# The FFN weights of a transformer block, laid out by quads in memory

## The chip, the cores and the metric

One NeuronCore of one Trainium2 chip runs the whole kernel. The metric is the time of one execution on the device in microseconds (us), the median of several runs. Its engines are TensorE (PE; its weight loads are listed apart as PEld), VectorE (DVE), ScalarE (ACT), GpSimd (POOL) and SyncE (SP); sixteen DMA engines move data between the main memory (HBM) and the on-chip memory, and they serve the queues of SP and POOL alike.

## The reference

One block with 256 tokens of width 2048, all in float32: a mixer of two kinds of attention, an output projection, and a feed-forward network (FFN) of width 5632. Only the last needs to be seen here:

```python
D_FF = -(-8 * D_MODEL // (3 * 256)) * 256          # 5632
...
    h = h + merged @ w_out[l]
    hn = rms_norm(h, norm_ffn_g[l])
    h = h + (jax.nn.silu(hn @ w_ffn_gate[l]) * (hn @ w_ffn_up[l])) @ w_ffn_down[l]
```

`w_ffn_gate` and `w_ffn_up` are 2048 x 5632, `w_ffn_down` is 5632 x 2048: 138 MB in all, each byte read once.

## The kernel before

**Products.** The kernel keeps the accuracy of float32 with three matmuls on a faster format. Each weight is split into a high and a low part (`u_hi`, made by ACT in L1134; `u_lo`, made by DVE in L1675), the activations likewise, and high by high, high by low (L2226, L2227) and low by high (L2231) are added in PSUM. The function `product` (L2220) does this for one unit: eight matmuls with the high part of the weights, then, after a wait on `lo_ready`, four with the low part, each with 128 x 512 weights moving past a loaded block of activations.

**Units, quads and panels.** A quad is the raw float32 block that one load brings: 4 row tiles of 128 rows, by 512 columns (`UNIT_KT = 4`, `COLS = 512`), 1 MB, held as 128 partitions of 8 KB. Six buffers `quad0` to `quad5` take them in turn. A unit is a quad, or a sum of quads, that is split and multiplied. A panel is a pair of column blocks of 512 over 2048 rows. Its first 2 x 2 quads (11, 12, 21, 22) are multiplied by a Strassen-like scheme with seven products, the units M1 to M7; the remaining four quads are the plain units N0 to N3, each multiplied by both halves of the tokens. The sums of quads that the scheme needs are made on DVE (L1683, L1689, L1694) and, one for each panel, by an accumulating DMA that POOL issues (L918, `quad<-quad`): quad 22 is added onto quad 12, for unit M7. The FFN has 17 panels: 11 of kind `gu`, whose two halves are the same column block of gate and up, and 6 of kind `down`, in three blocks (4, 4 and 3 `gu` panels, after each two `down` panels). The order of the units is written out by hand (`ORDER`, `SHORT_ORDER`); `plan_panels` builds the panels from the number of column blocks of the FFN, and `plan_loads` gives each load its buffer and the event that frees it.

**Loads.** The weights come on SP's queue. `load_quad` (issue in L815) first waits until DVE has made the low part, or the last sum, of what lay in the buffer (`quad_freed`), then issues one DMA. Its source is the weight matrix as the caller has it, rows apart by the full width of the matrix; the view `(k p) n -> p k n` makes partition p take row p of each of the four row tiles:

```python
                src = w[0, row0:row0 + UNIT_KT * P, col0:col0 + COLS].rearrange("(k p) n -> p k n", p=P)
                sp.dma_start(panel.stage.quad[slot][:].rearrange("p (k n) -> p k n", n=COLS), src).then_inc(panel.stage.landed[slot], 16)
```

So a partition reads four runs of 512 floats (2 KB). On SP nothing but further loads stands behind an FFN load, and after the last of them the read of the partial output (L860). ACT waits for the landing in `unit_hi` (L1134), DVE in its sums, POOL before L918.

**The other DMAs of this stage.** The results of the `down` panels leave PSUM through ACT (`evac`, L1299) and POOL adds them to the output in memory by accumulating DMAs (L947, `out<-evac`). The residual h is loaded once as 2 MB, x in rows of 8 KB (L853).

Of the kernel before, what the change touches and what calls it, by code (L numbers as in the profile page):

```python
# [27 lines left out]
P = 128  # L28
COLS = 512
# [9 lines left out]
UNIT_KT = 4  # L39
# [165 lines left out]
def single(kind, col, kt, letter="O"):  # L205

    panel = Panel(-1, kind, col, kt, None)
    for i in range(kt // UNIT_KT):
        panel.add_unit(f"{letter}{i}", f"{letter}{i}", i * UNIT_KT)
    return panel  # L210


def plan_out(kt, n, first_index):

    third_out = single("out", 2, kt, "U")
    panel = Panel(n, "out2", 0, kt, None)
    panel.i = -1
    panel.add_products()
    for a, name in enumerate(OUT_ORDER):
        u = (third_out if name[0] == "U" else panel).unit[name]  # L220
        u.index = first_index + a
        panel.order.append(u)
    return third_out, panel
# [44 lines left out]
def plan_panels(kt, ff_cols, d_cols, first_index, first_n):  # L268

    last_out = single("out", d_cols - 1, kt)  # L270
    panels = []

    def panel(kind, col, kts):
        panels.append(Panel(first_n + len(panels), kind, col, kts, panels[-1] if panels else None))
        panels[-1].i = len(panels) - 1
        panels[-1].add_products()
        return panels[-1]

    down = 0
    for block, ff in enumerate(range(0, ff_cols, FF_BLOCKS)):  # L280
        k = min(FF_BLOCKS, ff_cols - ff)
        for i in range(k):
            p = panel("gu", ff + i, kt)
            p.block, p.block_slot = block, i
        for m in range(d_cols // 2):
            p = panel("down", m, k * GROUP)
            p.block, p.row, p.down = block, ff * GROUP, down
            down += 1
    index = first_index
    for p in panels:  # L290
        short = p.kind == "down" and p.col == 0 and p.kts < kt
        for name in SHORT_ORDER if short else ORDER if p.i else FIRST_ORDER:
            owner = p.prev if name[-1] == "-" else last_out if name[0] == "O" else p
            if name[0:2] in owner.unit:
                p.order.append(owner.unit[name[0:2]])
        if p is panels[-1]:
            p.order += [p.unit[name] for name in ("N2", "N3") if name in p.unit]
        for u in p.order:
            u.index = index
            index += 1  # L300
    return last_out, panels
# [54 lines left out]
def build(nc, x, norm_mix_g, w_in, q_norm_a, k_norm_a, sink_a, t5_bias, q_norm_b, k_norm_b, rel_bias_b,  # L356
# [3 lines left out]
    KT = D // P  # L360
    NB = D // COLS
# [11 lines left out]
    PIECES = jobs[-1].piece0 + jobs[-1].pieces  # L373
# [10 lines left out]
    last_slots = dict(zip(b_units[-4:], ((3, 1), (2, 0), (0, 2), (3, 0))))  # L384
    b_hi_free, b_lo_free = plan_splits(b_units, B0, B0, B0 + 4, (), B0 + 4, last_slots)
    third_out, outs = plan_out(KT, len(heads) + len(branches), PIECES)
    last_out, panels = plan_panels(KT, w_ffn_gate.shape[2] // COLS, NB, PIECES + len(outs.order), outs.n + 1)
    units = outs.order + [u for panel in panels for u in panel.order]
    loads, _ = plan_loads(units, [PIECES - 2 * RAW_SLOTS + 2 * slot + 2 for slot in range(RAW_SLOTS)] + [0, 1])
    H_SETS = 1 + max(j.set for j in jobs if j.set is not None)  # L390
# [10 lines left out]
    with ExitStack() as ctx:  # L401
# [319 lines left out]
        def _(sp):  # L721
# [3 lines left out]
            def quad_freed(freed):  # L725
                if freed[0] == "sum":
                    sp.wait_ge(sum_ready, sums(freed[1], "Z"))
                else:
                    sp.wait_ge(lo_ready, freed[1] + 1)
# [47 lines left out]
            def load_quad(load):  # L777

                panel, name, slot, freed = load.panel, load.name, load.slot, load.freed
                if freed is None and panel.stage is q_stage:  # L780
                    if slot < RAW_SLOTS:
                        sp.wait_ge(lo_ready, 2 * RAW_SLOTS + 2 * slot + 2)
                elif freed is None and panel.stage is b_stage:
                    if slot < RAW_SLOTS:
                        sp.wait_ge(lo_ready, B0 - 2 * RAW_SLOTS + 2 * slot + 2)
                    else:
                        sp.wait_ge(piece_used, B0)
                elif freed is None:
                    if slot < RAW_SLOTS:
                        sp.wait_ge(lo_ready, PIECES - 2 * RAW_SLOTS + 2 * slot + 2)  # L790
                    else:
                        sp.wait_ge(piece_used, after_branch.piece0)
                else:
                    quad_freed(freed)
                if panel.kind == "out":
                    w, row0, col0 = w_out, load.kt0 * P, panel.col * COLS
                elif panel.kind == "out2":
                    w, row0, col0 = w_out, load.kt0 * P, (2 * panel.col + load.half) * COLS
                elif panel.kind == "v":
                    w, row0, col0 = w_in, load.kt0 * P, head_col("v", panel.col)  # L800
                elif panel.kind == "gb":
                    w, row0, col0 = w_in, load.kt0 * P, QA + 2 * KVA + 3 * QB + D + panel.col * COLS
                elif panel.kind == "ba":
                    w, row0, col0 = w_branch_a, load.kt0 * P, (2 * panel.col + load.half) * COLS
                elif panel.kind == "heads":
                    w, row0 = w_in, load.kt0 * P
                    col0 = head_col(*panel.halves[load.half])
                elif panel.kind == "gu":
                    w, row0 = (w_ffn_gate, w_ffn_up)[load.half], load.kt0 * P
                    col0 = panel.col * COLS  # L810
                else:
                    w, row0 = w_ffn_down, (panel.row + load.kt0) * P
                    col0 = (2 * panel.col + load.half) * COLS
                src = w[0, row0:row0 + UNIT_KT * P, col0:col0 + COLS].rearrange("(k p) n -> p k n", p=P)
                sp.dma_start(panel.stage.quad[slot][:].rearrange("p (k n) -> p k n", n=COLS), src).then_inc(panel.stage.landed[slot], 16)  # L815

            def head_col(kind, n):

                if kind == "v":
                    return QA + 2 * KVA + 2 * QB + n * COLS  # L820
                return n * COLS if n < QA // COLS else 2 * KVA + n * COLS

            def do_job(j):
                if j is jobs[2]:
                    for load in q_loads:
                        load_quad(load)
                if j is after_branch:
                    for c, load in enumerate(b_loads):
                        load_quad(load)
                        i = att_step(jobs[2], 2 * c + B0 - ATT_PIECE0, 6)  # L830
                        if i // 2 < NATT:
                            load_bias(i // 2)
                for q in range(j.pieces // 2):
                    if j.prev is None:
                        load_first(j, 2 * q)
                        load_first(j, 2 * q + 1)
                    else:
                        load_chunk(j, q)
                    i = att_step(j, 2 * q, 6)
                    if i >= 0 and i // 2 < NATT:  # L840
                        if i == 0:
                            sp.wait_ge(table_stored, 16)
                            sp.wait_ge(masks_ready, 1)
                        load_bias(i // 2)
# [4 lines left out]
            for c, load in enumerate(loads):  # L849
                load_quad(load)  # L850
                if c == H_AFTER:
                    sp.wait_ge(merged, NB)
                    sp.dma_start(h[:], x_view).then_inc(h_landed, 16)  # L853
# [1693 lines left out]
    return (np.arange(buckets)[:, None] == bucket[None, :]).astype(np.float32)  # L2547


# [14 lines left out]
```

## Time and profile before

| | us |
|---|---|
| median of 3 runs | 1275.11 (1274.64 to 1275.16) |
| the profiled execution | 1275.66 |
| its span, first to last instruction | 1273.9 |
| PE busy | 1267.6 |
| DVE busy | 1041.1 |
| ACT busy | 749.8 |
| granted TensorE clock | 1.0 of full speed throughout |

The profile lists every instruction with its start and duration, the DMA packets, and for each idle stretch of an engine the event that ended it. Busy times overlap between engines. Matmuls are pipelined: their records are longer (0.39 us) than the distance from one to the next, so for PE it is the distance that tells the pace.

### The profile page before, as it was taken

The numbers are of one execution on the slowest core, as the hardware profiler recorded it, in microseconds if no ns is written. First come the engines' busy times: TensorE is split into PE (matmuls) and PEld (weight loads), VectorE is DVE, ScalarE is ACT, GpSimd is POOL, SyncE is SP. The second block draws the span as 40 slices with busy tenths as digits, with TensorE's granted clock in tenths as the row PEclk, the third lists the DMA queues.
The fourth block names the chain that finished last, engine by engine and source line by source line (L and its number), as shares of the span: only waits on it lengthen the run. The fifth ranks groups of instructions, "written<-read, shape, count | busy, mean of one in ns | idle before, by whom it ended". The sixth has DMA issues, their size and how long they took to land.

```text
span 1273.9 us, 15071 instructions
## 1 busy us (share of the span) xinstructions
PE 1267.6 (100%) x5925; PEld 1044.0 (82%) x5925; DVE 1041.1 (82%) x932; ACT 749.8 (59%) x761; POOL 80.6 (6%) x71
## 2 busy tenths in 40 slices
PE   9999999999999999999999999999999999999999
PEld 7888887777788888888888888888888888888887
DVE  5888787778897577868989887878898888888996
ACT  5776566665675454556656655656565655556653
POOL 1212230000000000001000000000000001000000
DMA  7876747553675766956786669877877689866874
GB/s 250 306 230 201 238 129 228 156 155 119 191 252 174 242 224 206 320 208 186 243 278 218 201 196 287 256 244 207 260 227 252 185 245 285 253 213 195 282 219 121
DMA packets 137589, 282.88 MB, mean 222 GB/s; under 512 B 5344, under 2 KB 13856, under 8 KB 134320
## 3 DMA queue, kind: packets, MB, share of 16 engines
q1 hardware_dynamic: 130624, 250.37, 56.6%
q0 software_dynamic: 6896, 31.55, 13.1%
q8 instruction: 47, 0.77, 0.2%
q14 instruction: 22, 0.18, 0.0%
HBM read 249.38 MB, written 8.41 MB: 202 GB/s over the span
## 4 chain that ended last, share of the span: by engine, by line
PE 95%; DVE 2%; ACT 1%; issue 1%; DMA 0%; POOL 0%; SPq 0%; DVEq 0%; ACTq 0%
PE bank L2226 25%; PE bank L2231 25%; PE bank L2227 25%; PE bank L2166 6%; PE bank L2167 5%; PE bank L2174 5%; PE bank L2115 1%; DVE u_lo L1675 1%; PE bank L2142 1%; PE bank L2384 1%; PE bank L2127 1%; DMA x_rows<-in_x 0%; PE bank L2100 0%; ACT u_hi L1134 0%; PE bank L2090 0%
## 5 line engine op out<-in xcount | busy, mean ns | idle before, releaser
L1675 DVE TENSOR_TENSOR u_lo<-quad,u_hi 128x2048 fp32r<-128x2048 f32 x237 | 538.5, 2288 | 107.0 <-ACT u_hi L1134 57.1
L1134 ACT ACTIVATE u_hi<-quad 128x2048 fp32r<-128x2048 f32 x242 | 459.9, 1915 | 276.5 <-PE bank L2231 154.5
L2226 PE MATMUL bank<-u_hi,xT_hi 128*128 128x512 f32 x644 | 251.0, 390 | 0.0
L2227 PE MATMUL bank<-u_hi,xT_lo 128*128 128x512 f32 x644 | 250.6, 389 | 0.0
L2231 PE MATMUL bank<-u_lo,xT_hi 128*128 128x512 f32 x696 | 186.3, 389 | 0.0
L2231 PEld LDWEIGHTS bank<-u_lo,xT_hi 128*128 128x128 f32 x696 | 130.5, 188 | 27.4 <-DVE u_lo L1675 0.3
L2226 PEld LDWEIGHTS bank<-u_hi,xT_hi 128*128 128x128 f32 x644 | 120.9, 188 | 25.3 <-issue 0.3
L2227 PEld LDWEIGHTS bank<-u_hi,xT_lo 128*128 128x128 f32 x644 | 120.9, 188 | 25.0
L1430 DVE TENSOR_TENSOR w_lo<-raw,w_hi 128x1024 fp32r<-128x1024 f32 (+1 forms) x80 | 92.9, 1170 | 53.2 <-ACT w_hi L979 51.3
L979 ACT ACTIVATE w_hi<-raw 128x1024 fp32r<-128x1024 f32 (+1 forms) x80 | 80.4, 1016 | 89.5 <-PE bank L2174 77.2
L2166 PE MATMUL bank<-w_hi,xT_hi 128*128 128x512 f32 (+1 forms) x256 | 99.4, 392 | 0.0
L2167 PE MATMUL bank<-w_hi,xT_lo 128*128 128x512 f32 (+1 forms) x256 | 95.7, 378 | 0.0
L2227 PE MATMUL bank<-u_hi,fT_lo 128*128 128x512 f32 (+1 forms) x236 | 90.7, 385 | 0.0
L2226 PE MATMUL bank<-u_hi,fT_hi 128*128 128x512 f32 (+1 forms) x236 | 90.7, 385 | 0.0
L2226 PE MATMUL bank<-u_hi,xs_hi 128*128 128x512 f32 x216 | 85.0, 394 | 0.7 <-DVE bank L1705 0.7
L2227 PE MATMUL bank<-u_hi,xs_lo 128*128 128x512 f32 x216 | 84.1, 389 | 0.0
L918 POOL DMA_DIRECT2D quad<-quad x23 | 20.4, 886 | 825.9 <-DVE quad L1683 639.8
L2174 PE MATMUL bank<-w_lo,xT_hi 128*128 128x512 f32 (+1 forms) x256 | 65.2, 377 | 0.0
L2231 PE MATMUL bank<-u_lo,fT_hi 128*128 128x512 f32 (+1 forms) x236 | 62.2, 385 | 0.0
L2231 PE MATMUL bank<-u_lo,xs_hi 128*128 128x512 f32 x224 | 59.9, 389 | 0.0
L2166 PEld LDWEIGHTS bank<-w_hi,xT_hi 128*128 128x128 f32 x256 | 48.2, 188 | 10.3 <-issue 0.6
L2167 PEld LDWEIGHTS bank<-w_hi,xT_lo 128*128 128x128 f32 x256 | 48.3, 189 | 7.8
(277 smaller groups left out, 1845.8 us busy)
## 6 DMA issues: line engine op xcount, KB each, us to landing
quad<-in_w_ffn_gate SPq DMA_DIRECT2D x44, 1024.0 KB, 6.8
quad<-in_w_ffn_up SPq DMA_DIRECT2D x44, 1024.0 KB, 6.2
quad<-in_w_ffn_down SPq DMA_DIRECT2D x44, 1024.0 KB, 6.2
quad<-in_w_in SPq DMA_DIRECT2D x33, 1024.0 KB, 6.4
raw<-in_w_in SPq DMA_DIRECT2D x24, 1024.0 KB, 5.6
quad<-quad POOLq DMA_DIRECT2D x23, 1024.0 KB, 8.2
quad<-in_w_out SPq DMA_DIRECT2D x16, 1024.0 KB, 6.0
raw<-in_w_branch_b SPq DMA_DIRECT2D x8, 1024.0 KB, 5.3
```

Source lines behind the costliest of these rows:

```text
L918: pool.dma_start(st.quad[panel.slot["12"]][:], st.quad[panel.slot["22"]][:], accum_op=ALU.add).then_inc(q_summed, 16)
L979: A(w_hi[:, p % SPLIT_SLOTS, 0:w], raw[:, c % RAW_SLOTS, (k % 2) * w:(k % 2 + 1) * w], ACT.Copy).then_inc(hi_ready, 1)
L1134: A(st.hi[u.hi][:], st.quad[slot][:], ACT.Copy).then_inc(hi_ready, u.step)
L1430: V.tensor_tensor(w_lo[:, p % SPLIT_SLOTS, 0:w], raw[:, (j.chunk0 + k // 2) % RAW_SLOTS, (k % 2) * w:(k % 2 + 1) * w], w_hi[:, p % SPLIT_S ...
L1675: V.tensor_tensor(st.lo[u.lo][:], st.quad[u.panel.slot[u.raw]][:], st.hi[u.hi][:].bitcast(F32), ALU.subtract).then_inc(lo_ready, u.step)
L2115: ins = M(dst, qT[rows, b * PAIRS + n, tokens(t)], k, start=True, stop=True)
L2166: M(sums, hi[:, j.kt0 + kt, tokens(t)], w_hi[:, p % SPLIT_SLOTS, w], start=kt == 0, stop=False)
L2167: M(sums, lo[:, j.kt0 + kt, tokens(t)], w_hi[:, p % SPLIT_SLOTS, w], start=False, stop=False)
L2174: ins = M(sums, hi[:, j.kt0 + kt, tokens(t)], w_lo[:, p % SPLIT_SLOTS, w], start=False, stop=kt == j.kts - 1)
L2226: M(sums, a_hi(k), hi[:, w], start=start and k == 0, stop=False, skip_group_check=True)
L2227: M(sums, a_lo(k), hi[:, w], start=False, stop=False, skip_group_check=True)
L2231: ins = M(sums, a_hi(k), lo[:, w], start=False, stop=k == UNIT_KT - 1, skip_group_check=True)
```

## The change

The three FFN weights are passed as arrays of another shape, made on the host before the launch: (column blocks of 512, row quads of 512 rows, 128, 2048). Entry [c, r, p] holds, one behind the other, row p of each of the four row tiles of quad (c, r). `load_quad` takes one such entry for a `gu` or `down` panel and copies it as it lies: 128 partitions of 8 KB, 1 MB in one piece. The number of column blocks of the FFN, formerly the width by 512, is read from the first size of the new array. All other weights are loaded as before.

```diff
@@ -384,7 +384,7 @@
-    last_out, panels = plan_panels(KT, w_ffn_gate.shape[2] // COLS, NB, PIECES + len(outs.order), outs.n + 1)
+    last_out, panels = plan_panels(KT, w_ffn_gate.shape[0], NB, PIECES + len(outs.order), outs.n + 1)
@@ -806,11 +806,14 @@
                 elif panel.kind == "gu":
-                    w, row0 = (w_ffn_gate, w_ffn_up)[load.half], load.kt0 * P
-                    col0 = panel.col * COLS
+                    sp.dma_start(panel.stage.quad[slot][:], (w_ffn_gate, w_ffn_up)[load.half][panel.col, load.kt0 // UNIT_KT]
+                                 ).then_inc(panel.stage.landed[slot], 16)
+                    return
                 else:
-                    w, row0 = w_ffn_down, (panel.row + load.kt0) * P
-                    col0 = (2 * panel.col + load.half) * COLS
+                    sp.dma_start(panel.stage.quad[slot][:],
+                                 w_ffn_down[2 * panel.col + load.half, (panel.row + load.kt0) // UNIT_KT]
+                                 ).then_inc(panel.stage.landed[slot], 16)
+                    return
@@ -2547,6 +2550,13 @@
+def by_quad(w):
+
+    rows, cols = w.shape
+    tiles = w.reshape(rows // (UNIT_KT * P), UNIT_KT, P, cols // COLS, COLS).transpose(3, 0, 2, 1, 4)
+    return np.ascontiguousarray(tiles.reshape(cols // COLS, rows // (UNIT_KT * P), P, UNIT_KT * COLS))
...
+        if name in ("w_ffn_gate", "w_ffn_up", "w_ffn_down"):
+            a = by_quad(a[0])
```

## Rows read from the trace of the kernel before

**Rows 1.** The page, busy time of each engine, share of the span, instructions.
```profile
PE 1267.6 (100%) x5925; PEld 1044.0 (82%) x5925; DVE 1041.1 (82%) x932; ACT 749.8 (59%) x761; POOL 80.6 (6%) x71
```
**Rows 2.** Windows: length, busy PE, PEld, DVE, ACT, POOL, clock, DMA share, GB/s.
```profile
540.00:1274.00 734.00, 730.96 (x3294) 606.22 (x3292) 620.28 (x363) 426.65 (x314) 30.91 (x33) 1.00 0.73 229
1100.00:1125.00 25.00, 25.00 (x112) 20.71 (x111) 18.17 (x9) 13.61 (x12) 2.09 (x2) 1.00 1.05 326
1255.00:1270.00 15.00, 15.00 (x76) 12.74 (x75) 8.62 (x9) 1.71 (x1) 1.21 (x1) 1.00 0.36 75
```
**Rows 3.** Chain of waits in time, 1104 to 1113 us: start, length, what.
```profile
1106.43 0.91 PE bank L2231 x4
...
1109.15 0.91 PE bank L2231 x4
```
**Rows 4.** The same chain, 1256 to 1266 us.
```profile
1256.39 0.91 PE bank L2231 x4
...
1259.11 0.91 PE bank L2231 x4
```
**Rows 5.** The chain by line, 540 us to the end.
```profile
by line: PE bank L2231 32.6%; PE bank L2226 32.6%; PE bank L2227 32.5%; PE bank L2384 1.3%; PE bank L2397 0.5%; DVE part L2046 0.1%; issue 0.0%
```
**Rows 6.** Waits of PEld, 540 us to the end: total, times, longest.
```profile
PEld bank L2226 <- issue: 0.7, 2, 0.5
```
**Rows 7.** Waits of SP's queue, same stretch and columns.
```profile
SPq L815 <- DVE u_lo L1675: 643.7, 117, 16.2
```
**Rows 8.** L815, 540 to 1274 us (ns of an issue, landings); last, the load at 611.4.
```profile
L815 SPq DMA_DIRECT2D quad<-in_w_ffn_gate x43: 367/368/368, 563.1 to 1162.4; - x43
...
DMA to landing us min/median/max: 4.9/6.3/12.1
...
DMA to landing us min/median/max: 8.6/8.6/8.6
```
**Rows 9.** Timeline of ACT, DVE and PE around that load's unit: start, length.
```profile
620.07 1.92 ACT L1134 ACTIVATE u_hi<-quad 128x2048 fp32r<-128x2048 f32 x1
617.51 6.81 DVE L1675 TENSOR_TENSOR u_lo<-quad,u_hi 128x2048 fp32r<-128x2048 f32 x3
631.15 0.84 PE L2231 MATMUL bank<-u_lo,xT_hi 128*128 128x512 f32 x3
```
**Rows 10.** The page's DMA issues: KB each, median us to landing.
```profile
quad<-in_w_ffn_gate SPq DMA_DIRECT2D x44, 1024.0 KB, 6.8
quad<-quad POOLq DMA_DIRECT2D x23, 1024.0 KB, 8.2
h<-in_x SPq DMA_DIRECT2D x1, 2048.0 KB, 7.4
```
**Rows 11.** The page's DMA packets and queues: packets, MB, share of 16 engines.
```profile
DMA packets 137589, 282.88 MB, mean 222 GB/s; under 512 B 5344, under 2 KB 13856, under 8 KB 134320
q1 hardware_dynamic: 130624, 250.37, 56.6%
q8 instruction: 47, 0.77, 0.2%
q14 instruction: 22, 0.18, 0.0%
```
**Rows 12.** Landing of L918's at 1112.5; of all of L947; waits for L947.
```profile
DMA to landing us min/median/max: 10.0/10.0/10.0
...
DMA to landing us min/median/max: 5.7/10.7/12.7
...
ACT side_a L1281 <- DMA out<-evac: 7.9, 2, 4.0
```
**Rows 13.** Timeline of ACT, DVE and PE around that panel's M7: start, length.
```profile
1126.95 1.91 ACT L1134 ACTIVATE u_hi<-quad 128x2048 fp32r<-128x2048 f32 x1
1132.08 2.28 DVE L1675 TENSOR_TENSOR u_lo<-quad,u_hi 128x2048 fp32r<-128x2048 f32 x1
1139.83 0.85 PE L2231 MATMUL bank<-u_lo,xs_hi 128*128 128x512 f32 x3
```

## The prediction, made before the change was run

> **What bounds the kernel now.** I read the page from the top, then only the second half of the run, since that is where the changed loads are issued. The busy times come first [rows 1]: the matmul stream of TensorE (PE) covers 1267.6 of 1273.9 us, and no other engine is near that. A busy PE can still hide small holes, so the next thing to look at is the pace. In the chain of waits, followed in order of time, groups of four low-part matmuls stand 2.72 us apart while the DMA engines are at their busiest [rows 2, 3] (1106.43 and 1109.15). With the eight matmuls of the high part in between, twelve take 2.72 us, or 227 ns each. In the last 20 us, when no more weights are loaded, the same groups stand at 1256.39 and 1259.11 [rows 4]: 2.72 us again. The DMA share was 1.05 in the first stretch and 0.36 in the second [rows 2]. The pace of PE thus doesn't depend on what the DMA engines do.
>
> Next, who PE waits for. From 540 us to the end the chain is PE for 32.6 + 32.6 + 32.5 + 1.3 + 0.5 = 99.5% [rows 5]; no DMA is named in it. In the same stretch the list of waits has for the PE side one line: 0.7 us in all, in two pieces, released by no DMA [rows 6]. The loads themselves wait: SyncE's queue (SP), which issues them, spent 643.7 of these 734 us until VectorE (DVE) had finished with a buffer [rows 7]. The supply is paced by the consumer.
>
> How far ahead the supply runs is the cover that hides everything below. I looked for the load that leaves the least. It is the one issued at 611.4 us (panel 0, unit N3), which took 8.6 us to land [rows 8], so it was there at 620.0. ScalarE (ACT) began the unit's high part at 620.07 and ended at 621.99; DVE's run of three low parts, of which this unit's is the last, ended at 624.32; PE began the unit's low products at 631.15 [rows 9], and its eight high ones, at 0.227 us each, 1.8 us before, at 629.3. The load has 0.0 us to spare against ACT, yet the split weights lie ready 7.3 us (high) and 6.8 us (low) before PE asks for them. The slowest landing of the whole stage, 12.1 us [rows 8], belongs to no unit that is closer than this.
>
> **The change part by part.** What is computed, the order of units, buffers and waits stay as they are: the first size of the new gate array is the number of column blocks, which is what the old expression gave (5632 / 512 = 11). Only the source side of 132 loads (44 for each of the three weights [rows 10]) is another. Each still moves 1 MB and ends in one count on the same semaphore.
>
> Packets: a load of a quad has 128 partitions times 4 runs of 2 KB, 512 packets; laid out by quads it has 128 runs of 8 KB. That a run of 8 KB goes as one packet is borne out by a count: 137589 packets in all less 134320 under 8 KB leave 3269 [rows 11]. The 23 sums between two quads (128 partitions of 8 KB) make 2944, the one load of h (2 MB in rows of 8 KB) 256, the two instruction queues 47 + 22 = 69; together 3269 exactly [rows 10, 11]. So the hardware queue loses 132 x (512 - 128) = 50688 packets: 130624 become 79936.
>
> Time of a load: now 4.9 to 12.1 us, median 6.3 [rows 8]. The nearest row for runs of 8 KB from memory on the same queue is the load of h, 2 MB in 7.4 us [rows 10]; it too reads one contiguous block. If the rate per byte is that of the 2 KB runs, the quickest 1 MB load (4.9) and this one give 2.5 us for a further MB and 2.4 us that don't depend on size; that is a consistent pair, and it would leave the landing at 4.9 at best. If nothing were fixed, 1 MB would take 3.7. So a load gains between nothing and 1.2 us of its quickest time; I take the end near nothing, since 2.5 us per MB is already far quicker than the 326 GB/s that the busiest stretch reaches [rows 2]. The median should come to 5 to 6.3 us. On the path this is worth 0: the loads' landing is hidden by the 6.8 us and more of split weights ahead of PE [rows 9]. The cover would be gone if a load took 6.8 us longer than now, and then it would cost the excess.
>
> Issue: one instruction of 0.37 us per load on SP now [rows 8]. With a simpler pattern it costs between nothing and that. SP waits 643.7 us in the stage [rows 7], so 132 x 0.37 = 49 us saved or doubled vanish in its waits. Behind a load on SP stand only further loads and, at the end, the read of the partial output; a quicker issue starts nothing earlier, since each load is released by DVE.
>
> DMA time: the hardware queue's packets take 56.6% of 16 engines' span, 0.566 x 16 x 1273.9 / 130624 = 88 ns each [rows 11]. The changed loads have 67584 of them, 5970 us of engine time or 29% of the span. With the quickest load's 4.9 going to between 4.9 and 3.7, the share falls by 0 to 7 points; I expect 53 to 57% for the queue. PE doesn't wait for it: 0.
>
> The queue beside it: GpSimd (POOL) issues the sums of two quads (accumulating DMAs, 8.2 us to landing [rows 10]) and the sums into the output (10.7 us [rows 12]). They share the 16 engines with the loads, and the loads' pieces are now four times as large. At worst a sum stands behind one whole further load, 4.9 us. The sum issued at 1112.5 landed 10.0 us later, at 1122.5 [rows 12]; its reader, ACT's high part of M7, began at 1126.95, DVE ended the low part at 1134.36, and PE came to it at 1139.83 [rows 13]. The sum may be 4.4 us later before ACT notices, and DVE's result lies ready for 5.5 us more: cover 9.9 us against 4.9. The 17 quad sums of the stage are like it. The sums into the output held ACT up at one of its two lines for 7.9 us in all, at most 4.0 [rows 12], and such waits come out of the same lead of ACT over PE, 6.8 us and more, where 4.9 fits. Cost 0.
>
> The sum: against the profiled execution, 1273.9 us of span and 1.8 us around it make 1275.66. Change 0.0 from landings, 0.0 from issue, 0.0 from the other queue. That execution is 0.55 us above the median of the runs, 1275.11, so I forecast **1275.1 us**. What is left to come and go is the little that isn't pace: at most the 0.7 us of waits [rows 6] down, and about 1 us up for a unit that comes late once.
>
> **The rivals.**
> *Faster: the pace of PE has memory waits in it.* Of 734.0 us the weight loads of PE are busy for 606.2 [rows 2], which leaves 127.8 us. If these were waits for memory that the DMA engines cause, they would shrink with the DMA time, at most by 1.2 / 4.9 = 24%: 31 us, 1244 us. Against it stands the equal pace of 2.72 us at DMA shares of 1.05 and 0.36 [rows 2 to 4]; this alone holds such an effect under 0.01 us in 2.72. A gain of over 0.2% (2.6 us, about what a measurement of this kernel can tell from no change) would need a mechanism that I don't see. Chance 2%. The Trainium skill has the rule that makes this worth a rival: Perfetto Trace Analysis, Identifying the Most-Contended Engine, holds the matmul's busy time for a bad measure and wants the busy share of the weight loads judged instead. By that rule the kernel has 18% of headroom, not 0%. The trace has the 82%, and no wait in it that a DMA ends.
>
> *Slower: larger packets hold up the accumulating DMAs.* With 8 KB on either side a sum that alternates with loads gets a smaller share of an engine. It decides from the point where a quad sum lands 9.9 us later than now, 18 us and not 8.2. At 12 us later it would cost 2.1 us for each of the 17 panels of this stage, 36 us: 1311 us. For it: ACT already waits for these DMAs [rows 12]. Against it: a load has 1 MB in all, so no more than 4.9 us can be put ahead of a sum unless two loads are queued together, and 9.8 us is still within the cover. Chance 2%. The Trainium skill, in DMA: Bandwidth & Descriptors, Queues, rings and completion order, says that a DMA engine goes round its queues packet by packet; that is the mechanism by which larger packets would shift the shares. The trace of before doesn't show it one way or the other.
>
> *The change doesn't do what it says.* The contiguous 8 KB could be cut up again, or the block of 1 MB be spread over the engines in another way. Then the packets stay at 130624 and the landings at 6.3 us, or fall elsewhere between 5 and 12 us, and the time is the same 1275.1. Chance 3%.
>
> **How the numbers follow.** The forecast has 93%, the case of unchanged packets 3%, faster 2%, slower 2%. The first two are both no change: 96%. The range need not reach to the rivals: 0.7 us down and 1 us up from the terms above, and the spread of the runs (1274.64 to 1275.16) doubled, give 1273.9 to 1276.6.
>
> **What would show it.** In the profile of the changed kernel the hardware queue should have 79936 packets, the packets under 8 KB should be 66736, the landings of the FFN weights should be no longer than now, and the groups of four should still stand 2.72 us apart. The chain from 540 us on should be PE for over 99%. I am wrong if PE's pace in the FFN differs from 2.72 us, if PE or its weight loads wait for DVE or ACT by more than 2 us in all, or if the quad sums land more than 9.9 us later.

## The result, and the profile after

The changed kernel takes 1279.70 us (median of 6 runs, 1279.25 to 1283.6) against 1275.13 for the kernel before (6 runs, 1274.64 to 1275.78). The ratio is 1.0039, 95% interval 1.0029 to 1.005: 4.6 us or 0.4% slower. The forecast was no change, with a range that ended at 1276.6. Five of the six runs lie between 1279.25 and 1280.04; the sixth, 1283.6, is the only one whose mean granted TensorE clock is under 1.0 (0.999); `same_place_runs` below has more on that.

The table below puts the profiled execution of the changed kernel beside that of the kernel before. Its lines have moved: L815 became L809 (gate, up) and L813 (down), L918 is L921, L947 is L950, L1281 is L1284, L1299 is L1302, L2226 and L2231 are L2229 and L2234.

| | before | after |
|---|---|---|
| span, us | 1273.9 | 1278.2 |
| the profiled execution, us | 1275.66 | 1280.04 |
| PE busy, us | 1267.6 | 1268.3 |
| hardware queue: packets, share of 16 engines | 130624, 56.6% | 79936, 54.2% |
| output sums `out<-evac`, median to landing, us | 10.7 | 12.2 |

First the page of the changed kernel: its packets and queues. The 79936 packets of the hardware queue and the 66736 under 8 KB are the numbers worked out beforehand from [rows 11].

```profile
DMA packets 86901, 282.88 MB, mean 221 GB/s; under 512 B 5344, under 2 KB 13856, under 8 KB 66736
...
q1 hardware_dynamic: 79936, 250.37, 54.2%
```

Next the landings in the stage of the FFN. The first line is of the loads of gate and up (L809), the second of those of down (L813), the third of the quad sums (L921), the last of the output sums (L950).

```profile
DMA to landing us min/median/max: 4.7/6.3/9.6
...
DMA to landing us min/median/max: 4.7/5.5/9.6
...
DMA to landing us min/median/max: 7.9/8.7/10.0
...
DMA to landing us min/median/max: 5.8/12.2/13.4
```

The slowest loads became quicker (12.1 to 9.6 us) and the quickest a little (4.9 to 4.7); the median was 6.3 us over all loads [rows 8] and is now 6.3 for gate and up and 5.5 for down. The output sums, which the change doesn't touch, became 1.5 us slower ([rows 12] had 5.7/10.7/12.7).

The waits from 540 us on, with total, times and longest, are the lines that tell where the time went:

```profile
ACT side_a L1284 <- DMA out<-evac: 13.2, 2, 6.7
ACT evac L1302 <- DMA out<-evac: 10.9, 2, 5.6
PEld bank L2229 <- issue: 4.8, 6, 1.7
PE bank L2229 <- issue: 2.5, 2, 1.3
```

ACT waited 7.9 us for output sums in the first of these lines before [rows 12], and 13.2 now. The second line stood like this in the kernel before:

```profile
ACT evac L1299 <- DMA out<-evac: 7.2, 2, 3.8
```

The weight loads of PE, which had 0.7 us of waits in two pieces [rows 6], have 4.8 in six, and the matmuls 2.5 in two. (The two lines lie over each other: a hole in the one is a hole in the other.) The chain of waits, by line and then in order of time, names the two longest holes:

```profile
by line: PE bank L2229 32.6%; PE bank L2234 32.5%; PE bank L2230 32.4%; PE bank L2387 1.3%; PE bank L2400 0.5%; issue 0.4%; DVE part L2049 0.1%
...
867.90 1.29 issue
1118.34 1.22 issue
```

Here is the first of them in the timeline, start and length in us. In the kernel before, the output sum issued at 854.1 landed after 10.6 us, and this followed:

```profile
864.78 0.69 ACT L1281 ACTIVATE side_a<-bank,h_rs 128x512 f32<-128x512 f32 x1 [3.86 <-DMA out<-evac]
...
865.99 1.07 PE L2231 MATMUL bank<-u_lo,xT_hi 128*128 128x512 f32 x4
866.90 0.39 PE L2226 MATMUL bank<-u_hi,xT_hi 128*128 128x512 f32 x1
```

In the changed kernel the same sum was issued at 855.0 and landed after 13.4 us:

```profile
868.41 0.69 ACT L1284 ACTIVATE side_a<-bank,h_rs 128x512 f32<-128x512 f32 x1 [6.65 <-DMA out<-evac]
...
866.84 1.07 PE L2234 MATMUL bank<-u_lo,xT_hi 128*128 128x512 f32 x4
869.20 0.47 PE L2229 MATMUL bank<-u_hi,xT_hi 128*128 128x512 f32 x1 [1.29 <-issue]
```

The reader is to see two things. ACT's instruction is `gate_opened`: it reads PSUM bank 0 of the finished panel into `side_a`. Since `side_a` shares its memory with `evac`, the tile that the output sum is being read from, ACT must wait for the sum's landing. PE begins the next panel in bank 0 and waits until ACT has read it (`gate_ready`). And the cover there was small: before, ACT was done at 864.78 + 0.69 = 865.47 and PE came at 866.90; after, PE followed 0.10 us behind ACT's end (869.10 and 869.20). So a delay of 1.43 - 0.10 = 1.3 us would have cost nothing, and the sum landed 2.8 us later. At the other three places of the same sort (output sums issued near 814, 1064 and 1105 us) it is the same wait, in two of them with `evac` itself as the tile to be emptied into (L1302). Before, ACT and then PE at these three:

```profile
823.95 0.60 ACT L1299 ACTIVATE evac<-bank 128x512 f32<-128x512 f32 x1 [3.84 <-DMA out<-evac]
826.10 0.39 PE L2226 MATMUL bank<-u_hi,xT_hi 128*128 128x512 f32 x1
...
1071.96 0.60 ACT L1299 ACTIVATE evac<-bank 128x512 f32<-128x512 f32 x1 [3.40 <-DMA out<-evac]
1074.54 0.39 PE L2226 MATMUL bank<-u_hi,xT_hi 128*128 128x512 f32 x1
...
1113.38 0.69 ACT L1281 ACTIVATE side_a<-bank,h_rs 128x512 f32<-128x512 f32 x1 [4.02 <-DMA out<-evac]
1115.34 0.39 PE L2226 MATMUL bank<-u_hi,xT_hi 128*128 128x512 f32 x1
```

After, ACT alone; PE came at 826.84, 1077.25 and 1119.55, 0.10 us behind ACT's end each time:

```profile
826.14 0.60 ACT L1302 ACTIVATE evac<-bank 128x512 f32<-128x512 f32 x1 [5.37 <-DMA out<-evac]
...
1076.55 0.60 ACT L1302 ACTIVATE evac<-bank 128x512 f32<-128x512 f32 x1 [5.57 <-DMA out<-evac]
...
1118.77 0.69 ACT L1284 ACTIVATE side_a<-bank,h_rs 128x512 f32<-128x512 f32 x1 [6.57 <-DMA out<-evac]
```

The cover isn't the same at each place. It is the distance from ACT's end to PE's start before, less the 0.10 us that stays:

| output sum issued near | ACT waits longer by, us | cover, us | over the cover, us |
|---|---|---|---|
| 814 | 5.37 - 3.84 = 1.53 | 1.55 - 0.10 = 1.45 | 0.08 |
| 854 | 6.65 - 3.86 = 2.79 | 1.43 - 0.10 = 1.33 | 1.46 |
| 1064 | 5.57 - 3.40 = 2.17 | 1.98 - 0.10 = 1.88 | 0.29 |
| 1105 | 6.57 - 4.02 = 2.55 | 1.27 - 0.10 = 1.17 | 1.38 |

Together that is 3.2 us in this pair of executions, nearly all of it at the two places of `side_a`.

The two transfers that traded places can be seen side by side. The load of `up` issued 0.3 us after that output sum took 11.5 us before and 8.7 us after; the sum took 10.6 and 13.4. Before, the load and then the sum:

```profile
DMA to landing us min/median/max: 11.5/11.5/11.5
...
DMA to landing us min/median/max: 10.6/10.6/10.6
```

After, in the same order:

```profile
DMA to landing us min/median/max: 8.7/8.7/8.7
...
DMA to landing us min/median/max: 13.4/13.4/13.4
```

### The profile page after: what moved, and what is told of

Its sections match the earlier page's. It is cut to its first block, busy times and chain, and to the rows that moved or that the text cites. A ratio compares the mean times of both kernels' runs of the same rounds, so it can differ in the third digit from the quotient of the medians.

```text
span 1278.2 us, 15071 instructions
## 1 busy us (share of the span) xinstructions
PE 1268.3 (99%) x5925; PEld 1043.4 (82%) x5925; DVE 1040.7 (81%) x932; ACT 749.1 (59%) x761; POOL 80.6 (6%) x71
## 2 busy tenths in 40 slices
DMA packets 86901, 282.88 MB, mean 221 GB/s; under 512 B 5344, under 2 KB 13856, under 8 KB 66736
## 3 DMA queue, kind: packets, MB, share of 16 engines
q1 hardware_dynamic: 79936, 250.37, 54.2%
q0 software_dynamic: 6896, 31.55, 13.1%
## 4 chain that ended last, share of the span: by engine, by line
PE 95%; DVE 2%; issue 1%; ACT 1%; DMA 1%; POOL 0%; SPq 0%; DVEq 0%; ACTq 0%
PE bank L2229 25%; PE bank L2234 25%; PE bank L2230 25%; PE bank L2169 6%; PE bank L2170 5%; PE bank L2177 5%; PE bank L2118 1%; DVE u_lo L1678 1%; PE bank L2145 1%; PE bank L2130 1%; PE bank L2387 1%; DMA x_rows<-in_x 1%; PE bank L2103 0%; ACT u_hi L1137 0%; PE bank L2093 0%
## 5 line engine op out<-in xcount | busy, mean ns | idle before, releaser
L2229 PE MATMUL bank<-u_hi,xT_hi 128*128 128x512 f32 x644 | 251.3, 390 | 2.6 <-issue 2.5
L2234 PE MATMUL bank<-u_lo,xT_hi 128*128 128x512 f32 x696 | 186.3, 389 | 0.0
L2234 PEld LDWEIGHTS bank<-u_lo,xT_hi 128*128 128x128 f32 x696 | 130.6, 188 | 27.4 <-DVE u_lo L1678 0.3
L2229 PEld LDWEIGHTS bank<-u_hi,xT_hi 128*128 128x128 f32 x644 | 120.9, 188 | 29.3 <-issue 4.5
L2229 PE MATMUL bank<-u_hi,fT_hi 128*128 128x512 f32 (+1 forms) x236 | 90.7, 385 | 0.0
L2229 PE MATMUL bank<-u_hi,xs_hi 128*128 128x512 f32 x216 | 85.1, 394 | 0.7 <-DVE bank L1708 0.7
L921 POOL DMA_DIRECT2D quad<-quad x23 | 20.4, 886 | 829.1 <-DVE quad L1686 642.5
L2234 PE MATMUL bank<-u_lo,fT_hi 128*128 128x512 f32 (+1 forms) x236 | 62.2, 385 | 0.0
L2234 PE MATMUL bank<-u_lo,xs_hi 128*128 128x512 f32 x224 | 60.0, 389 | 0.0
```

What stands on the lines that cost most here:

```text
L921: pool.dma_start(st.quad[panel.slot["12"]][:], st.quad[panel.slot["22"]][:], accum_op=ALU.add).then_inc(q_summed, 16)
L2229: M(sums, a_hi(k), hi[:, w], start=start and k == 0, stop=False, skip_group_check=True)
L2234: ins = M(sums, a_hi(k), lo[:, w], start=False, stop=k == UNIT_KT - 1, skip_group_check=True)
```

## The experiments

Theory A: the loads' larger packets take more of each turn on the DMA engines, so an output sum beside them lands later, ACT empties bank 0 later, and PE begins the next panel late. Theory B: it isn't the packets but the place, one contiguous megabyte read where the output sums read and write. Theory C: the output sums have nothing to do with it. Each time stands beside that of the kernel before from the same session.

**The place or the packet.** `block_2k` keeps every quad in one contiguous megabyte but orders it by row tile, so that the runs are 2 KB again:

```diff
-                    sp.dma_start(panel.stage.quad[slot][:], (w_ffn_gate, w_ffn_up)[load.half][panel.col, load.kt0 // UNIT_KT]
+                    sp.dma_start(panel.stage.quad[slot][:].rearrange("p (a n) -> p a n", n=1 * COLS),
+                                 (w_ffn_gate, w_ffn_up)[load.half][panel.col, load.kt0 // UNIT_KT].rearrange("a p n -> p a n")
```

> Each quad still lies in one contiguous block of 1 MB, but row tile by row tile, so that a load has 512 runs of 2 KB again. Theory A (packet size: an output sum shares the DMA engines packet by packet with the loads, and a load's packets of 8 KB take more of each turn): 130624 packets on the hardware queue, output sums land in a median of 10.7 us as before the change, PE never waits beyond the 0.7 us of before, time 1275.1 us. Theory B (place in memory: reading 1 MB from one place disturbs the output sums' reading and writing of the same memory): landings of 12 to 13 us stay, time 1279.7. Theory C (the loss has nothing to do with the output sums): 1279.7 with PE's pace changed somewhere.

Measured: 1275.26 us (11 runs) against 1275.28, ratio 1.0 (0.9991 to 1.0009). The hardware queue has 130624 packets, the output sums a median of 10.9 us. The loss is gone with the megabyte still in one place, so theory B falls as the cause of the 4.6 us. In the profiled execution the sums at the two `side_a` places landed late all the same (12.4 and 11.9 us after their issue). Whether that is scatter or a small effect of the place isn't shown; the median time has none of it. PE's side waited 1.6 us there instead of 0.7:

```profile
ACT side_a L1284 <- DMA out<-evac: 10.9, 2, 5.7
ACT evac L1302 <- DMA out<-evac: 7.4, 2, 3.9
PEld bank L2229 <- issue: 1.6, 4, 0.7
```

`block_4k` has two runs of 4 KB for each partition in the same megabyte (the edit is as above with `n=2 * COLS`).

> The same contiguous block of 1 MB, with two runs of 4 KB for each partition: 96832 packets on the hardware queue. Theory A: the output sums land between the two cases, 11.3 us in the median, and since ACT and PE have about 1.2 us of cover there, most of the loss is gone: 1275.3 to 1276.5 us. Theory B: 1279.7, as with 8 KB. A loss that grows evenly with the packet size would give 1276.7 to 1277.5.

Measured: 1275.99 us (11 runs) against 1275.28, ratio 1.0007 (0.9998 to 1.0015); 96832 packets, output sums in 11.3 us. The time lies 0.7 us up, within the range expected of theory A and below the 1276.7 to 1277.5 of a loss that grows evenly with the packet; with a cover, the first part of a delay costs nothing. The interval alone doesn't part it from no change.

`same_place_runs` takes the arrays of the changed kernel and writes the same copy as four runs of 2 KB:

```diff
-                    sp.dma_start(panel.stage.quad[slot][:], (w_ffn_gate, w_ffn_up)[load.half][panel.col, load.kt0 // UNIT_KT]
+                    sp.dma_start(panel.stage.quad[slot][:].rearrange("p (a n) -> p a n", n=COLS),
+                                 (w_ffn_gate, w_ffn_up)[load.half][panel.col, load.kt0 // UNIT_KT].rearrange("p (a n) -> p a n", n=COLS)
```

> The arrays are those of the changed kernel; only the DMA is written as four runs of 2 KB for each partition, which lie one behind the other. If these are joined to packets of 8 KB all the same, 79936 packets on the hardware queue and 1279.7 us under every theory. If they stay 2 KB (130624 packets): theory A 1275.1 us, theory B 1279.7 us.

Measured: 79936 packets and 1280.70 us (6 runs, 1278.44 to 1287.38) against 1275.28, ratio 1.0049 (1.0032 to 1.0066). The four runs, which lie one behind the other on both sides, went as one packet, so these are the transfers of the changed kernel once more, and the loss is there again. It says nothing on A against B.

It shows something else. The profiled execution is the slowest of the six, 1287.38 us, with the same packets as the changed kernel's 1280.04. Its output sum issued at 813.4 took 14.4 us to land, where the changed kernel's took 12.1, and PE had four long holes, of 2.19, 0.91, 2.24 and 1.84 us. Soon after the first and the last of these the granted TensorE clock was at half, 1.2 GHz and not 2.4 (window, length, busy times, clock, DMA share, GB/s as in [rows 2]):

```profile
829.40:832.70 3.30, 3.30 (x9) 2.53 (x8) 2.29 (x1) 3.15 (x3) 1.22 (x1) 0.50 0.91 278
1126.40:1129.70 3.30, 3.30 (x10) 2.53 (x9) 2.29 (x1) 2.92 (x3) 0.00 (x0) 0.50 0.92 276
```

In these stretches matmuls stand 0.43 us apart and not 0.23; some eight of them, at 0.2 us more each, make an estimate of 1.6 us for each stretch. So a late output sum can cost twice: the hole, and the slower clock that followed some of the holes. The execution of 1283.6 us of the changed kernel has a mean clock of 0.999, as one such stretch would give; it wasn't traced.

**The way from the sum to PE.** `own_evac_8k` is the changed kernel with two `evac` tiles, one for each half, in the memory of `ms_hi`, which is free by then. ACT's waits for the sum before go:

```diff
-        evac = at("evac", [P, T, COLS], F32, o_stage)
...
+        evac = [at(f"evac{i}", [P, T, COLS], F32, o_ms + i * T * COLS * 4) for i in range(2)]
...
-                    if panel.block and panel.block_slot == 0:
-                        act.wait_ge(out_added1, 16 * downs_before(panel))
...
-                    if half:
-                        act.wait_ge(out_added0, 16 * (panel.down + 1))
-                    elif panel.prev.kind == "down":
-                        act.wait_ge(out_added1, 16 * panel.down)
-                    else:
+                    if panel.down:
+                        act.wait_ge((out_added0, out_added1)[half], 16 * panel.down)
+                    if not half and panel.prev.kind != "down":
```

> The changed kernel, but the two output sums of a down panel are issued from two tiles of their own, in memory that is free by then, so that ACT can empty the next PSUM bank without waiting for the sum before. If the loss runs over that wait (output sum lands late, ACT empties bank 0 late, PE begins the next panel late): the sums still land 12 us and more after their issue, ACT doesn't wait for them any more, PE has no idle time from it, 1275.1 to 1275.8 us. If the loss is elsewhere (quad sums, loads, the start of the kernel): 1279.7 us, or 1278 to 1279 for a part of it.

Measured: 1275.42 us (11 runs, 1274.91 to 1275.69) against 1275.28, ratio 1.0001 (0.9992 to 1.001). The output sums are as slow as ever, or slower; only nobody stands behind them. First their landings, then all that is left of waits on the PE side:

```profile
DMA to landing us min/median/max: 5.9/13.1/13.8
```
```profile
PEld bank L2226 <- issue: 0.7, 2, 0.5
```

This is the run that rules theory C out: all but 0.1 us of the loss passed through the waits that were taken away. Its control is the same edit with the loads of the kernel before, `own_evac_2k`:

> The kernel before with the two tiles of own_evac_8k: the control for that run. ACT's waits for output sums go, the sums land in 10.7 us, PE had lost nothing to them: 1275.2 us. If this were clearly below own_evac_8k (by 0.5 us or more), large packets would have a second cost that has nothing to do with the output sums.

Measured: 1274.99 us (11 runs) against 1274.98 in its session, ratio 1.0 (0.9991 to 1.0009). Large packets thus cost 0.1 us where nothing waits for an output sum, which is within the noise, and the waits cost the kernel before nothing that can be measured.

**The cover measured by itself.** `late_sums_2k` leaves the loads at 2 KB and puts an operation of GpSimd ahead of each output sum:

```diff
                 pool.wait_ge(evacuated, T * (panel.down + 1))
+                in_order(nc.gpsimd.tensor_tensor(q_rs[:], q_ms[:], minus_half[:], ALU.pow))
                 pool.dma_start(out_view[:, :, cs], evac[:], accum_op=ALU.add).then_inc(added, 16)
```

> The kernel before, with runs of 2 KB, and one operation of 1 to 5 us (median 2.9 us in the trace of before, L899) on GpSimd ahead of every output sum; nothing else is changed. This measures the cover at the disputed place by itself. If the way is output sum, ACT emptying bank 0, PE's next panel, with a cover of 1.2 to 1.3 us, four of the ten sums cost their delay less the cover, 1.6 us each and 6 to 7 us in all: 1281 to 1283 us. If the cover is 6.8 us, as the prediction had it: 1275.3 us.

Measured: 1277.20 us (11 runs, 1275.99 to 1278.05) against 1274.98, ratio 1.0017 (1.0008 to 1.0026): 2.2 us lost, a third of what was expected. The direction is that of the small cover, the size isn't. The trace says why. The sums were issued some 3 us later, but once issued they took 9.1 us in the median and not 10.7, probably since part of the loads beside them had gone by:

```profile
DMA to landing us min/median/max: 5.9/9.1/10.0
```
```profile
ACT side_a L1282 <- DMA out<-evac: 12.4, 2, 6.3
ACT evac L1300 <- DMA out<-evac: 10.8, 2, 5.5
```

Against [rows 12] ACT waited (12.4 - 7.9) / 2 = 2.2 us longer at each place of the first line, and (10.8 - 7.2) / 2 = 1.8 at each of the second (7.2 as above). The covers in the table above average 1.25 us at the former two and 1.67 at the latter two, so the sum is 2 x 1.0 + 2 x 0.1 = 2.2 us, beside 2.2 measured. So a delay of the sums alone, with small packets everywhere, costs PE time once it is over these covers.

**Which loads.** `only_gate_up` and `only_down` lay out only those weights by quads and load the others as before.

> Gate and up laid out by quads, down as before. The loads in flight beside the sums issued at 854 and 1102 us are all of gate and up, beside those at 813 and 1061 one of three or four is of down. Packet theory: these two sums still land 2.5 us later than before and cost 1.5 us each, 1278.5 to 1279.5 us. If every load with large packets counted alike, two thirds of the loss: 1278.2.

Measured: 1278.24 us (11 runs) against 1274.98, ratio 1.0023 (1.0014 to 1.0032): 3.3 us. That is 0.3 below the range of the packet theory and on the 1278.2 that was expected if every large load counted alike, so this run alone doesn't favour the former.

> Down laid out by quads, gate and up as before. Packet theory: no large packet is in flight beside the sums at 854 and 1102 us, which land in 10.6 us as before; the sums at 813 and 1061 meet one such load and land up to 1 us later, within the cover: 1275.3 us, at most 1275.8. If every load counted alike, a third of the loss: 1276.7.

Measured: 1275.36 us (11 runs) against 1274.98, ratio 1.0002 (0.9993 to 1.0011). PE's side waited 0.7 us as before. The two lines here are ACT's waits, which are those of the kernel before within 0.5 us each:

```profile
ACT evac L1301 <- DMA out<-evac: 8.2, 2, 4.1
ACT side_a L1283 <- DMA out<-evac: 7.8, 2, 3.9
```

The 1275.36 us are the value of the packet theory (1275.3) and not the 1276.7 of every load counting alike. Gate and up, two thirds of the loads, alone cost 3.3 of the 4.6 us, which is their share by number; down alone costs 0.4, a quarter of its share and within the noise. The two don't add up to 4.6, as is to be expected where the first part of each delay falls within a cover. That the loads beside the critical sums are what matters rests on `only_down`.

**The same from the other side.** If turns are taken packet by packet, smaller packets in the sums should do what larger ones in the loads did. `split_1k` and its control `split_2k` leave the loads at 2 KB and issue each output sum as two DMAs, split by columns (runs of 1 KB) or by tokens (runs of 2 KB); the counts that are waited for are doubled. The edit of `split_1k`:

```diff
-                pool.dma_start(out_view[:, :, cs], evac[:], accum_op=ALU.add).then_inc(added, 16)
+                for q in range(2):
+                    cols = slice(q * COLS // 2, (q + 1) * COLS // 2)
+                    pool.dma_start(out_view[:, :, cs][:, :, cols], evac[:, :, cols], accum_op=ALU.add).then_inc(added, 16)
```

> Control for split_1k: the kernel before, loads of 2 KB runs, with each output sum issued as two DMAs, one for each half of the tokens, in runs of 2 KB as before (256 packets in all). The second issue costs GpSimd about 1.2 us more (L947 was 1.2 us), of which up to 1.2 to 1.3 us are covered: 1275.2 to 1276.5 us.

Measured: 1275.04 us (11 runs) against 1275.06. ACT's waits are even shorter than in the kernel before, by 1.4 and 0.8 us in all, perhaps because the first of the two DMAs can start moving while the second is being made; that wasn't tested.

> As split_2k, but the two DMAs are the two halves of the columns, in runs of 1 KB: 512 packets for each output sum, 5120 in place of 2560 in all. The loads keep 2 KB. If the queues take turns packet by packet, a sum with twice as many turns lets twice as many load packets by and lands 1 to 2 us later than in split_2k, which costs 1 us or more at each of the two worst places and less at two others: 1277 to 1279.5 us. If the engines are shared by bytes, its packets cost only their own overhead, and the time is that of split_2k within 0.5 us.

Measured: 1275.92 us (11 runs, 1275.14 to 1276.78) against 1275.06, ratio 1.0008 (0.9999 to 1.0017), 0.9 us above its control. ACT's waits in `split_2k`:

```profile
ACT side_a L1282 <- DMA out<-evac: 6.5, 2, 3.4
ACT evac L1300 <- DMA out<-evac: 6.4, 2, 3.2
```

and in `split_1k`:

```profile
ACT side_a L1283 <- DMA out<-evac: 11.0, 2, 5.7
ACT evac L1301 <- DMA out<-evac: 9.0, 2, 4.6
```

The sums end 2.2 and 1.3 us later at the two sorts of place, about as expected by turns. The time met neither range: it is 1.1 us under the 1277 to 1279.5 of the turns and 0.4 over what sharing by bytes allowed (within 0.5 of the control). A part of the delay is GpSimd's own: at the four critical places its two issues take 2.4 us together and 1.75 in the control. So this run agrees with the turns but doesn't prove them.

`joint_sum_8k` goes back to loads of 8 KB and makes one sum of the two of a `down` panel: one tile of 128 x 2 x 1024, one DMA of 1 MB in runs of 4 KB, issued when both halves are there.

> Loads by quads with 8 KB runs; the two output sums of a down panel are one DMA of 1 MB in 4 KB runs from a tile of its own, so five sums with as many packets (256) as each of the ten had. By turns: as many turns as half the bytes had, so it lands 13 to 15 us after its issue; by bytes, more like twice the variable part, 18 us and up. Nobody waits for it except the end of the kernel: 1275.2 to 1275.7 us, and at least the end must not wait (the last sum is now issued near 1255 us, and the last output is stored at 1271).

Measured: 1286.38 us (4 runs) against 1275.06, ratio 1.0091 (1.0077 to 1.0105). On the DMA it went nearly as the turns say: twice the bytes in the same number of packets landed in 15.2 us in the median, beside 13.1 for the half in `own_evac_8k`; 13 to 15 were expected by turns and 18 and up by bytes. That nobody waits was plainly wrong. With one tile for both halves, the next `down` panel of a block can't be emptied before the sum of the last has landed:

```profile
ACT evac L1296 <- DMA out<-evac: 17.1, 2, 8.6
PEld bank L2223 <- issue: 7.7, 4, 3.6
PE bank L2223 <- issue: 6.2, 2, 3.2
```

The holes and the clock behind them share the loss. First the two holes of PE in the chain, then the windows after them, with the clock third from the end:

```profile
825.76 3.04 issue
1079.12 3.17 issue
...
830.00:833.40 3.40, 3.40 (x10) 2.61 (x9) 2.42 (x2) 2.98 (x4) 0.00 (x0) 0.51 1.02 287
1082.70:1086.00 3.30, 3.30 (x10) 2.53 (x9) 1.98 (x1) 3.30 (x3) 0.00 (x0) 0.50 1.03 288
```

The two holes are 6.2 us of the 9.5 by which this execution's span exceeds the one before (1283.4 and 1273.9), and the two stretches at half clock, 1.6 us each by the estimate above, make 3.2. All four executions have a mean clock of 0.996 or 0.997. So the run shows the price of the same wait when it is longer, and that the clock behind each hole cost half as much again here.

## Why the prediction was wrong, point by point

**What bounds the kernel.** Right: PE at a fixed pace of 2.72 us for twelve matmuls, with the DMA engines busy or not. The pace is unchanged after; the loss is holes in it at four places, two of them long. By its own sign the prediction was wrong all the same: it allowed 2 us of waits of PE's side in all, and there are 4.8. The other two signs, another pace and quad sums 9.9 us later, didn't come.

**Packets and loads.** Right: 79936 packets and 66736 under 8 KB, to the last one; the queue's share 54.2%, within 53 to 57; landings of 4.7 to 9.6 us with medians of 6.3 and 5.5, within 5 to 6.3. The case that the packets stay as they were is out by the same count, and no version was faster than the kernel before.

**Issue on SP, PE waiting for loads.** Right: an issue went from 0.37 to 0.33 us, and PE waits for no load.

**The queue beside it.** The mechanism was named and the delay bounded rightly: at most 4.9 us was allowed, and 1.5 us came in the median and 2.8 at the worst place. For the quad sums the cover held too: their median in this stage went from 8.2 to 8.7 us and nobody lost by it.

**The step that failed** is the last sentence but one of that paragraph, on the output sums: "such waits come out of the same lead of ACT over PE, 6.8 us and more". That lead is the lead of split weights, taken from another place. Behind ACT's wait for an output sum stands no split but the reading of PSUM bank 0, in which PE begins its next panel; there the cover is 1.2 to 1.9 us. The rows for it were there to be read in the trace of before: ACT ended its read at 865.47 and PE came at 866.90. The sum of the change should have had, for each of the four places, the delay less the cover there. With the waits of the changed kernel that is the 3.2 us of the table, where 4.6 were measured between the medians and 4.4 between the two profiled executions. So "Cost 0" was the wrong term. The size of the delay couldn't be read from the trace of before; the bound of 4.9 us, put against this cover, would have said that a loss is possible.

**The slower rival** was priced at the wrong one of the two sums. It was said to decide from 9.9 us of delay of the quad sums, and was given 2% for it; it decides from 1.2 to 1.9 us of delay of the output sums. With that point against the bound of 4.9 us it would have deserved far more than 2%.

**What stays open.** About 0.5 us of the difference of the profiled executions lies in the first 9 us of the kernel, which the change doesn't touch: PE waited 0.81 us for `x_rows` before and 1.80 after. Since `own_evac_8k`, with the same arrays and loads, is within 0.1 us of the kernel before, I take it for scatter of one execution; that wasn't tested by itself. PE was 0.7 us behind just ahead of the first place (the same four low products begin at 825.19 before and 825.86 after) and 4.3 at the end (the two spans), so 3.7 us were lost from there on. The table has 3.2 of them. A few tenths more are in the restart, where the second matmul behind each hole comes 0.31 us after the first and not 0.23. Taken so, 0.9 of the 4.6 us between the medians has no place. The holes differ between executions, as `same_place_runs` shows, and each kernel has one trace. No version beat the kernel before: `own_evac_2k` and `split_2k` equal it.

## What to carry to other kernels

When a change speeds up one stream of transfers, look at those that share the engines with it: here larger packets made the slowest loads quicker (12.1 to 9.6 us) and the output sums beside them slower (10.7 to 12.2). For each of those, find who waits for its landing and what stands behind the waiting instruction, and read the cover at that very place, from the end of the released instruction to the start of its reader; a lead found elsewhere in the pipeline is no cover for it. Where the cover is small, a tile of its own can take the wait off the path: with it the slow sums of `own_evac_8k` cost 0.1 us.

## What the runs showed of the hardware

Two transfers in flight together traded time almost evenly: with packets of 8 KB and not 2 KB the load beside the sum landed 2.8 us earlier (11.5 to 8.7) and the sum 2.8 us later (10.6 to 13.4), while the queue's total time fell only from 56.6 to 54.2%. The last output sum, issued at 1255.4 us before and 1259.7 after, when no FFN load is in flight any more, landed in 5.7 and 5.8 us. The Trainium skill, in DMA: Bandwidth & Descriptors, Queues, rings and completion order, says that an engine goes round its queues packet by packet. The block, split and joint runs agree with it, but don't prove it. Its packet is a group of typically 9 to 17 descriptors, while the profile of these loads counts a packet for each contiguous run, so which unit the turns go by isn't shown.

Four runs of 2 KB which lie one behind the other on both sides went as one packet of 8 KB (79936 packets in `same_place_runs`); whether the build of the program or the DMA joins them isn't shown.

The granted TensorE clock fell to half (0.50 and 0.51) soon after holes of 3.04 and 3.17 us in `joint_sum_8k` and of 2.19 and 1.84 us in `same_place_runs`, but not after the holes of 0.91 and 2.24 us there nor after those of 1.29 and 1.22 us in the changed kernel. The length of the last hole alone thus doesn't decide it.
